# Plain float32 scores, an earlier output slab, a narrow norm and reordered tails in a transformer kernel

## The reference, cut to what matters

```python
# stick-breaking                                # dilated, merged over three branches
z = q @ k.T * hd**-0.5                          z = rope(q) @ rope(k).T * hd**-0.5
w = exp(log_sigmoid(z) + later log_sigmoid(-z)) p = softmax(z + log(count of branches))
# recurrent head, then its norm
o = o * rsqrt(mean(o*o, -1) + 1e-6) * g_norm * silu(g);  out = o @ w_out
```

## Time and profile before

| | |
|---|---|
| time, median of 3 runs | 2505.44 us (2505.25 to 2507.22) |
| profiled execution, its own time | 2502.9 us |
| its span, first to last instruction | 2501.1 us |
| TensorE matmul busy | 2433.5 us, 97% |
| VectorE, ScalarE, GpSimd busy | 1421.4, 925.1, 168.1 us |
| granted TensorE clock, mean | 0.995 |
| stick-breaking stage, dilated stage | about 8 to 219 us, 621 to 840 us |
| end of the recurrent stage, end of the window stage | 1545 to 1557 us, 2057 to 2086 us |

### The profile page before, as it was taken

How to read it: one execution, slowest core, us unless ns; L and a number is a source line. 1 busy time by engine, 2 the same in 40 slices (tenths; PEclk the granted TensorE clock), 3 DMA queues, 4 the chain that set the end, 5 groups by cost and what they waited for, 6 DMA issues and landing times.

```text
span 2501.1 us, 31542 instructions
## 1 busy us (share of the span) xinstructions
PE 2433.5 (97%) x11766; PEld 1985.7 (79%) x11766; DVE 1421.4 (57%) x2300; ACT 925.1 (37%) x1327; POOL 168.1 (7%) x179
## 2 busy tenths in 40 slices
PE   8999999999999999999999999999999998999998
PEld 6877888888777788888778887788888877888886
DVE  6775555433776464542266765766643665766634
ACT  5443322222767332222232332533321564433312
POOL 0000000000000000000020000000030462000031
PEclk9999999999999999999999999999999999999999
DMA  4212332223112233222222112232223312323232
GB/s 145 68 60 76 97 97 96 89 93 101 59 60 68 76 101 100 93 84 93 97 89 67 50 67 84 85 101 93 92 84 103 134 52 76 101 93 101 76 116 86
DMA packets 60792, 218.95 MB, mean 88 GB/s; under 512 B 6773, under 2 KB 7061, under 8 KB 60576
## 3 DMA queue, kind: packets, MB, share of 16 engines
q1 hardware_dynamic: 58608, 208.74, 25.8%
q0 software_dynamic: 2064, 8.97, 1.0%
q10 hardware_dynamic: 32, 0.02, 0.0%
HBM read 215.59 MB, written 2.12 MB: 87 GB/s over the span
## 4 chain that ended last, share of the span: by engine, by line
PE 89%; DVE 5%; ACT 4%; issue 1%; POOL 0%; DMA 0%; DVEq 0%; SPq 0%; ACTq 0%
PE ps L254 27%; PE ps L256 27%; PE ps L255 27%; PE ps L1832 2%; PE ps L1031 2%; PE ps L1006 1%; PE ps L1017 1%; ACT window_p L1501 1%; DVE wl L248 1%; ACT wh L240 1%; DVE stick_left L1221 1%; PE ps L1856 0%; DVE window_p L1563 0%; DVE stick_p L1227 0%; PE ps L1039 0%
## 5 line engine op out<-in xcount | busy, mean ns | idle before, releaser
L254 PE MATMUL ps<-xh,wh 128*128 128x512 f32 x2000 | 796.8, 398 | 17.3 <-DVE xl L460 8.6
L256 PE MATMUL ps<-xh,wl 128*128 128x512 f32 x2000 | 781.5, 391 | 0.0
L255 PE MATMUL ps<-xl,wh 128*128 128x512 f32 x2000 | 780.2, 390 | 0.0
L240 ACT ACTIVATE wh<-raw 128x1024 fp32r<-128x1024 f32 x332 | 348.8, 1055 | 499.2 <-PE ps L256 479.4
L248 DVE TENSOR_TENSOR wl<-raw,wh 128x1024 fp32r<-128x1024 f32 x332 | 409.6, 1235 | 188.4 <-ACT wh L240 188.2
L254 PEld LDWEIGHTS ps<-xh,wh 128*128 128x128 f32 x2000 | 376.8, 188 | 98.5 <-issue 12.7
L256 PEld LDWEIGHTS ps<-xh,wl 128*128 128x128 f32 x2000 | 376.3, 188 | 80.0
L255 PEld LDWEIGHTS ps<-xl,wh 128*128 128x128 f32 x2000 | 377.1, 189 | 76.9 <-issue 2.2
L254 PE MATMUL ps<-wh,up_ah 128*128 128x512 f32 x528 | 208.6, 395 | 1.0 <-DVE wl L404 1.0
L404 DVE TENSOR_TENSOR wl<-raw,wh 128x1024 fp32r<-128x1024 f32 x56 | 80.2, 1433 | 227.6 <-ACT wh L401 227.6
L255 PE MATMUL ps<-wl,up_ah 128*128 128x512 f32 x528 | 208.3, 395 | 0.0
(11 more groups left out here) (279 smaller groups left out, 3138.8 us busy)
## 6 DMA issues: line engine op xcount, KB each, us to landing
raw<-weights SPq DMA_DIRECT2D x388, 512.0 KB, 3.5
cst<-rows_d POOLq DMA_DIRECT2D x9, 512.0 KB, 4.8
hT<-x_t SPq DMA_DIRECT2D x8, 256.0 KB, 6.3
hgrn_mask<-levels POOLq DMA_DIRECT2D x1, 2048.0 KB, 7.9
window_bias<-bias_rows POOLq DMA_DIRECT2D x1, 2048.0 KB, 9.4
out_t<-hT SPq DMA_DIRECT2D x8, 256.0 KB, 2.2
cst<-consts SPq DMA_DIRECT2D x1, 832.0 KB, 8.7
cvt<-conv SPq DMA_DIRECT2D x1, 176.0 KB, 8.6
```

Of the source, the lines that this page charges most:

```text
L240: act.activation(wh[slot][:, :], raw[slot][:, :], ACT.Copy).then_inc(hi_done, 1)
L254: pe.matmul(out, w_hi, m_hi, start=first, stop=False, **kw)
L255: pe.matmul(out, w_hi, m_lo, start=False, stop=False, **kw)
L256: return pe.matmul(out, w_lo, m_hi, start=False, stop=last, **kw)
```

## The change

1. In the stick-breaking and dilated stage the scores are one plain float32 matmul per head and row block, from `qs` and `ks`, where they were three fp32r matmuls. The four splitting functions (`q_hi_act`, `k_hi_act`, `q_lo_dve`, `k_lo_dve`) and their tiles go. The scale 1/8 moves into the sigmoids and into the dilated query's rope.
2. At j = 6 ScalarE and VectorE split slab 24 directly behind slab 23, ahead of the next query; before, it came behind keys, queries and transposes (dilated) or behind the key's split (stick-breaking).
3. At j = 7 the early units are dealt out differently around the second transpose and the values: same units, another order.
4. After the last recurrent head the sum is taken with one column of ones into 128x4 (four matmuls), root and reciprocal work on 128x4, and four matmuls against the identity spread the result into PSUM, from where VectorE multiplies. These four stand between early units 20, 21 and 22, 23.
5. In the last step of the window stage, six further early units (for token block 3) run: one behind the first transpose, and five behind the values.

```diff
@@ heads_scores
-            pe.wait_ge(*a.q_ready(j + 1))
-            pe.wait_ge(*a.k_ready(j + 1))
+            pe.wait_ge(*a.qs_ready(j + 1))
+            pe.wait_ge(*a.ks_ready(j + 1))
-                for part in range(3):
-                    for hh in range(2):
-                        rows = slice(hh * HD, (hh + 1) * HD)
-                        qq, kk = (a.ql if part == 2 else a.qh)[rows, q], (a.kl if part == 1 else a.kh)[rows, 0:n]
-                        mm = pe.matmul(flat(3 * hh, 3 * hh + 3)[:, at:at + n], qq, kk, start=part == 0, stop=part == 2)
+                for hh in range(2):
+                    rows = slice(hh * HD, (hh + 1) * HD)
+                    mm = pe.matmul(flat(3 * hh, 3 * hh + 3)[:, at:at + n], a.qs[rows, q], a.ks[rows, 0:n],
+                                   start=True, stop=True)
@@ heads_pe, j = 7
-            for k, t in ((1, 0), (1, 1), (2, 0), (2, 1)):
+            for k, t in ((1, 0), (1, 1)):
                 o.early_unit(pe, k, t)
+            pe.wait_ge(*a.pt_ready(2 * j + 1))
+            for t in range(2):
+                o.early_unit(pe, 0, t, 2)
             heads_turn(pe, a, j, 1)
-            pe.wait_ge(*a.pt_ready(2 * j + 1))
-            for k, t in ((0, 0), (0, 1), (1, 0)):
-                o.early_unit(pe, k, t, 2)
+            for k, t, jj in ((1, 0, 2), (1, 1, 2), (2, 0, 0)):
+                o.early_unit(pe, k, t, jj)
             heads_values(pe, a, j)
-            for k, t in ((1, 1), (2, 0), (2, 1)):
-                o.early_unit(pe, k, t, 2)
+            for k, t, jj in ((2, 1, 0), (2, 0, 2), (2, 1, 2)):
+                o.early_unit(pe, k, t, jj)
@@ stick_act (dilated_act, stick_dve and dilated_dve alike)
                 heads_hi(act, a, 3 * j + 5)
+                if j == PAIRS - 2:
+                    heads_hi(act, a, 3 * j + 6)
                 if j + 1 < PAIRS:
-                    k_hi_act(act, a, j + 1)
-                    heads_hi(act, a, 3 * j + 6)
-                    q_hi_act(act, a, j + 1)
+                    if j < PAIRS - 2:
+                        heads_hi(act, a, 3 * j + 6)
@@ pe_head, after the last head
-                if not proj and 26 <= c < 30:
+                if not proj and 26 <= c < 28:
+                    hgrn_out_early(pe, c - 6)
+                if not proj and c == 28:
+                    pe.wait_ge(g.rs_ready, j + 1)
+                    for b in range(SB):
+                        mm = pe.matmul(ps[:, 5, token_block(b)], g.rs[:, b:b + 1].broadcast_to([P, P]), const("ident"),
+                                       start=True, stop=True)
+                    mm.then_inc(g.rs_spread, 1)
+                if not proj and 28 <= c < 30:
                     hgrn_out_early(pe, c - 6)
+                if not proj and c == 25:
+                    pe.wait_ge(g.sq_ready, j + 1)
+                    for b in range(SB):
+                        mm = pe.matmul(ps[:, 5, b:b + 1], g.sq[:, token_block(b)], ones[:, 0:1], start=True, stop=True)
+                    mm.then_inc(g.sum_done, 1)
@@ dve_head
+                n = S if proj else SB
+                dve.reciprocal(g.rs[:, 0:n], g.root[:, 0:n]).then_inc(g.rs_ready, 1)
+                    dve.wait_ge(g.rs_spread, 1)
+                    dve.tensor_tensor(g.og[:, :], g.og[:, :], ps[:, 5, :], ALU.mult).then_inc(g.gated, 1)
@@ win_out_early, j = 8
-                units = [(0, 0, 2), (0, 1, 2), (1, 0, 2)] if hh == 0 else [(1, 1, 2), (2, 0, 2), (2, 1, 2)]
+                units = [(0, 0, 2), (0, 1, 2), (1, 0, 2), (1, 1, 2)] if hh == 0 else [(2, 0, 2), (2, 1, 2), (0, 0, 3)]
+                if hh == 2:
+                    units = [(0, 1, 3), (1, 0, 3), (1, 1, 3), (2, 0, 3), (2, 1, 3)]
@@ window_pe
                 if j:
                     win_values_pe(pe, a, j - 1)
+                if j == PAIRS:
+                    win_out_early(pe, j, 2)
```

More of the change, by code:

```diff
@@ L1205, in take @@
             return dve.tensor_tensor(dst[:, :], ps[:, bank, :], rstd[:, :], ALU.mult)
[L1207 to L1214, removed]
         def stick_weights_dve(dve, a, j, hh):
@@ L1261, in rope_sin_dve @@
             s = a.swap[which]
-            dve.tensor_tensor(s[:, :], s[:, :], a.sinr[:, :], ALU.mult).then_inc(a.sin_done, 1)
-            dve.wait_ge(a.sin_done, n)
-            dve.tensor_tensor(dst[:, :], dst[:, :], s[:, :], ALU.add).then_inc(ready.sem, 1)
+            if which:
+                dve.tensor_tensor(s[:, :], s[:, :], a.sinr[:, :], ALU.mult).then_inc(a.sin_done, 1)
+                dve.wait_ge(a.sin_done, n)
+                dve.tensor_tensor(dst[:, :], dst[:, :], s[:, :], ALU.add).then_inc(ready.sem, 1)
+            else:
+                dve.scalar_tensor_tensor(out=s[:, :], in0=s[:, :], scalar=SCALE, in1=a.sinr[:, :], op0=ALU.mult,
+                                         op1=ALU.mult).then_inc(a.sin_done, 1)
+                dve.wait_ge(a.sin_done, n)
+                dve.scalar_tensor_tensor(out=dst[:, :], in0=dst[:, :], scalar=SCALE, in1=s[:, :], op0=ALU.mult,
+                                         op1=ALU.add).then_inc(ready.sem, 1)
         def heads_out_dve(dve, a, j):
@@ L1329, in dilated_dve @@
                 heads_lo(dve, a, 3 * j + 5)
+                if j == PAIRS - 2:
+                    heads_lo(dve, a, 3 * j + 6)
                 if j + 1 < PAIRS:
@@ L1885, in at_step @@
                     pe_hgrn_values(pe, g, i)
-                if attn and c == 25:
+                if not proj and c == 25:
[3 more added lines that the diff above has]
+                    mm.then_inc(g.sum_done, 1)
+                if attn and proj and c == 25:
                     pe.wait_ge(g.sq_ready, j + 1)
@@ L1944, in act_head @@
                 act.wait_ge(g.sum_done, j + 1)
-                act.activation(g.root[:, :], ps[:, 5, :], ACT.Sqrt, scale=1.0 / P,
+                n = S if proj else SB
+                act.activation(g.root[:, 0:n], ps[:, 5, 0:n], ACT.Sqrt, scale=1.0 / P,
                                bias=small[:, 0:1]).then_inc(g.root_ready, 1)
@@ L2020, in dve_head @@
                 dve.wait_ge(g.root_ready, j + 1)
-                dve.reciprocal(g.rs[:, :], g.root[:, :]).then_inc(g.rs_ready, 1)
+                n = S if proj else SB
+                dve.reciprocal(g.rs[:, 0:n], g.root[:, 0:n]).then_inc(g.rs_ready, 1)
                 dve.wait_ge(g.og_ready, j + 1)
-                dve.wait_ge(g.rs_ready, j + 1)
-                dve.tensor_tensor(g.og[:, :], g.og[:, :], g.rs[:, :], ALU.mult).then_inc(g.gated, 1)
+                if proj:
+                    dve.wait_ge(g.rs_ready, j + 1)
+                    dve.tensor_tensor(g.og[:, :], g.og[:, :], g.rs[:, :], ALU.mult).then_inc(g.gated, 1)
+                else:
+                    dve.wait_ge(g.rs_spread, 1)
+                    dve.tensor_tensor(g.og[:, :], g.og[:, :], ps[:, 5, :], ALU.mult).then_inc(g.gated, 1)
                 dve.wait_ge(g.gated, j + 1)
```

43 lines of the change are left out of this document (12 added, 31 removed).

## The result

The kernel after takes 2490.3 us (median of 4 runs, 2487.22 to 2491.84) where the kernel before took 2505.39 us beside it; the ratio is 0.9933, 95% interval 0.9919 to 0.9948. In a second set of runs it was 2488.71 us against 2507.11, ratio 0.9927 (0.9914 to 0.9940). The profiled execution took 2489.66 us, its span 2487.8 us, 13.3 us less than the 2501.1 of before.

What follows compares the result with a forecast made beforehand. The prediction took TensorE, 89% of the chain, as the bound. Gains of 19.3 us less 6.1 for the scores gave -13.2, 2489.7 us for the profiled execution; with the median 2.5 higher it predicted 2492 us, range 2486 to 2499.

Steps and rivals of the forecast that it cites:

- The terms for the waits: Heads stages, recurrent norm and window tail: shorter TensorE waits, -19.3 us together.
- The scores: Stick-breaking and dilated scores: plain float32 costs TensorE more than three fp32r parts, +6.1 us over 16 pairs (3.0 to 7.8).
- The term of 0.38 us a pair: Scores of one pair: a plain float32 group takes 2.50 us where the fp32r group takes 2.12.
- the high end: Scores: if two heads load one after the other, a group takes 2.61 us, 0.49 us more a pair.
- the price of 2.50: Scores: us taken for a plain float32 group, between 2.31 and 2.61, nearer to the recurrent rows.
- The splits: Four splitting steps removed: -1.5 us at the dilated start, -0.2 at the stick-breaking start, otherwise beside TensorE's projections.
- Slab 24: Pair 6 of both heads stages: an earlier split brings values earlier, -1.3 us stick-breaking, -6.9 us dilated.
- Stick-breaking tail: Last stick-breaking pair: reordered units cover the wait for slab 26 and avoid slow clock, -4.4 us.
- Dilated tail: Last dilated pair: no wait between the units, so the same units in another order give 0.
- no stretch at 0.50: Sign: no half-clock stretch in either heads stage behind its start, or behind the recurrent norm.
- the second rival: Shortened waits: the clock still falls or a next-late wait eats more, 4.2 us back, 2496 us; chance 0.20.
- Norm and window: Last recurrent norm: shorter reciprocal and full clock, -3.5 us. Window tail: five moved units cover a wait, -1.5 us.

Runs made afterwards that it cites:

- second set of runs: The kernel after once more, unchanged, beside the kernel before; 2488.71 us, ratio 0.9927; its profiled execution is the second one.
- Experiment 3: The kernel after with slab 24 split behind the queries again in both heads stages; 2498.31 us, ratio 0.9964 to the kernel before.
- experiment 4: The kernel after with the last recurrent norm on all 512 columns again; 2494.38 us, ratio 0.9947 to the kernel before.
- experiment 6: The kernel after with the old order of units in the last pair of both heads stages; 2493.39 us, ratio 0.9954 to the kernel before.
- experiment 12: The kernel after with the window stage's output units in the order before; 2492.94 us, ratio 0.9943 to the kernel before.
- Experiment 8: The kernel after with only the first 64 keys of each score product in pairs 1 to 7; one run, 2471.13 us.
- experiment 7: The kernel after with all four score products of the first head ahead of the second's; 2518.29 us, ratio 1.0045 to the kernel before.
- experiment 2: The kernel before with plain float32 scores, without the splits, and nothing else changed; 2505.52 us, ratio 0.9999 to the kernel before.
- experiment 1: The kernel after with the three fp32r score parts and their four splitting steps put back; 2494.2 us, ratio 0.9947 to the kernel before.
- a mixture: The kernel after with fp32r parts and splits in pairs 1 to 6, plain float32 in pairs 0 and 7; 2485.52 us, ratio 0.9916 to the kernel before.

## Why the prediction came out right, and where it was off

**The whole.** 2492 us was forecast and 2490.3 measured, inside the range. The terms for the waits hold one by one, and experiments 3, 4, 6 and 12 return four of them. That the profiled execution took 2489.66 us where the prediction wrote 2489.7 is luck: the scores cost 2.3 us less than priced and the first matmul came 1.0 us earlier, while the way to the first scores and the dilated tail took 1.8 and 1.65 us more.

**The scores, mis-sized.** The mechanism was right: the plain form costs more than the parts, the heads overlap, 2.13 us are streams. The term of 0.38 us a pair measured 0.24, and the +6.1 us were +3.8. What was off is the high end, "if two heads load one after the other, a pair of records takes at least 0.21 us", towards which the price of 2.50 was drawn. Experiment 8 shows that the 0.104 us read from the recurrent stage has the right size, but the two heads share it. The group is 2.13 + 0.23, the rest being its two ends. The same sharing undoes another reading: the fp32r pairs 0.11 us apart need not mean 0.055 us for each load, as the prediction has it, since two loads of 0.11 us side by side give the same spacing. So no row here contradicts one load time for both forms; no run tested fp32r by itself. The Trainium skill (TensorEngine Tiling (Array Packing), Key Properties) says that different tiles can execute weight loads and matmuls in parallel; experiments 7 and 8 agree, with 3.97 us against 2.36 and 0.11 us for a step of two heads.

**The splits.** -1.35 us at the dilated start against -1.5: `ks` alone ends the wait, as forecast. At the stick-breaking start the -0.2 is not shown: the way to the first scores was 1.6 us longer in the first profiled execution and 0.3 shorter in the second, and in experiment 2, which has no splits, it is as long as in the kernel before.

**Slab 24.** Both pairs 6 came out within 0.3 us, by the path that was named: `wl` early, `pt` next late, 1.82 us of wait where 2.0 was written, full clock after it. Experiments 1 and 3 show both halves of the term. Experiment 3 has wait and slow clock back, +6.6. In experiment 1 pair 6 waited 0.66 us longer and the clock fell; that is one execution, and no edge between the two waits follows from it.

**Stick-breaking tail.** -4.2 for -4.4, and experiment 6 gives it back in full.

**Dilated tail.** "Gives 0" is right for the order. The prediction also said that no stretch at 0.50 would come in either heads stage, and in the first profiled execution one did, behind a wait of 2.18 us which the kernel before has too. This is the second rival in part, at a place that it did not name and in some executions only.

**Norm and window.** -3.3 for -3.5, and -1.9 for -1.5. The extra 0.4 in the window stage is in part the 0.24 us before the second transposes, which the prediction did not see. The norm's wait fell by 2.8 us, but the spread stands in TensorE's own order now, so TensorE's start came forward by 1.9 and the clock gave the rest. Experiments 4 and 12 return both.

**What stays open.** The order of the units is no cause of the half-clock stretch in the dilated tail; what decides between two executions of one kernel was not found. So the clock parts of the gains (1.0 us in the dilated values, some 1.7 behind slab 26 and 1.4 behind the norm) rest on one profiled execution of each kernel and those of the experiments, where they came back.

## What to carry to other kernels

A change of form can cost the bound engine time and still pay through the waits it removes, so price it where the waits are: plain float32 scores paid at the dilated start and ahead of the last pair and cost 0.24 us everywhere else, which is why the landmarks put a mixture 2.9 us ahead. When a stall is moved, look for the one that is late next, as the prediction did with `pt`: 6.88 us became 1.82, not nothing. A stall can cost more than its length: one of 2.48 us was followed by 1.7 us of slow clock, those of 1.82 by none in eight executions, but those of 2.18 by some in three of twelve. And compare kernels by landmarks between like instructions: effects of 1 to 2 us stand out there when the times of whole runs differ by 3 us for one and the same kernel.

## What the runs showed that was not expected

**Half-clock stretches of one execution.** Nearly the same code, from 1240 to 1256 us, in the kernel after, then with the parts put back (there it stands 1.7 us later):

```profile
1240.00:1256.00 16.00, 13.39 (x59) 10.72 (x59) 10.17 (x18) 10.42 (x17) 0.00 (x0) 0.89 0.55 198
```

```profile
1240.00:1256.00 16.00, 12.66 (x57) 10.03 (x56) 10.45 (x19) 11.72 (x19) 1.00 (x2) 0.79 0.53 197
```

The mean clock is 0.89 in one and 0.79 in the other, and the way from the dilated output to the first recurrent product is 401.4 us in the first and 403.5 in the second. Over all thirteen profiled executions with full scores it is 401.3 to 402.3 us in eight and 403.3 to 403.6 in five; from the recurrent output to the window scores it is 408.1 in six and 409.5 to 409.8 in seven. Some 3.7 us of the spread between executions are these two places. The dilated start shows the same: the first group follows a wait of 1.12 to 1.15 us in twelve executions and is at half clock in one of them (experiment 7), and follows 2.52 and 2.53 us in two, at full clock in the kernel before and at half in experiment 1. The Trainium skill (TensorE: Matmul & The Clock Gate, The HAM clock gate) has the moment of a change hang on where the first work falls in a rhythm of the chip's own; two executions of one kernel with the same wait and another clock agree with that.

**Two heads for the price of one.** A step of two plain float32 records on the two row halves takes 0.11 us when little is streamed, as one record does; read as the load of the stationary block, two blocks of 64 rows and 128 columns load in the time of one, and a 128-key product hides them wholly. Alternating the two heads is worth 1.6 us in a group of 2.36.
